# Opening of a two-block transformer kernel: the order of four modulation quarters and two projection pieces, one quarter summed by two engines, and one sum ahead of an eviction

## The reference, cut to what matters

```
cond_act = jax.nn.silu(c)
ada = (cond_act @ w_ada + b_ada)[:, None, :]
sh1, sc1, g1, sh2, sc2, g2 = jnp.split(ada, 6, axis=-1)
u = layer_norm(x) * (1 + sc1) + sh1
proj = u @ w_in + b_in
```

## Time and profile before

| what | value |
|---|---|
| median of 3 runs | 2474.4 us (2473.87 to 2475.06) |
| the profiled execution: time | 2474.91 us |
| its span, first to last instruction | 2472.9 us |
| mean granted TensorE clock | 0.986 |
| TensorE matmul busy | 2322.6 us (94%) |
| VectorE busy | 1017.7 us (41%) |
| ScalarE busy | 356.3 us (14%) |
| chain that ended last | TensorE 73%, DMA 20%, VectorE 3%, ScalarE 2% |

### The profile page before, as it was taken

The page is one execution under the profiler, slowest core; times in us unless marked ns, Lnnn a source line. Parts: engine busy times, 40 slices in busy tenths (PEclk is TensorE's granted clock), DMA queues, the critical chain, the costliest instruction groups (busy, mean ns, idle before and its releaser), DMA issues.

```text
span 2472.9 us, 26320 instructions
## 1 busy us (share of the span) xinstructions
PE 2322.6 (94%) x10448; PEld 1373.8 (56%) x10448; DVE 1017.7 (41%) x2212; ACT 356.3 (14%) x725; POOL 31.8 (1%) x54
## 2 busy tenths in 40 slices
PE   6999999999999999999998998988899989989997
PEld 5878688458878685467554333333397533333332
DVE  4254656767556567223743111111245521111112
ACT  1211111001211110101532111111100011111111
POOL 0100000002000000000000000000000000000000
PEclk9999999999999999999998999999999989999999
DMA  9644868856267688532045999999954369999996
GB/s 313 255 153 171 306 248 291 305 193 234 98 248 257 218 326 303 187 119 85 35 185 228 430 429 429 428 429 428 417 197 170 122 241 429 429 428 429 428 429 290
DMA packets 160900, 701.04 MB, mean 283 GB/s; under 512 B 6064, under 2 KB 15536, under 8 KB 135216
## 3 DMA queue, kind: packets, MB, share of 16 engines
q1 hardware_dynamic: 158512, 691.49, 70.9%
q0 software_dynamic: 2304, 8.39, 1.0%
HBM read 694.61 MB, written 5.24 MB: 283 GB/s over the span
## 4 chain that ended last, share of the span: by engine, by line
PE 73%; DMA 20%; DVE 3%; ACT 2%; issue 1%; SPq 1%; DVEq 0%; ACTq 0%
PE banks L615 72%; DMA ring<-in_exp_w_down_dram 19%; ACT UT L1406 1%; DMA ring<-in_w_ada_dram 1%; PE banks L680 0%; DVE acc L1790 0%; PE banks L748 0%; DVE acc L1763 0%; ACT arena L1613 0%; SPq L2587 0%; DVE arena L2220 0%; DVE arena L2213 0%; DVE X L1872 0%; PE banks L1153 0%; PE banks L995 0%
## 5 line engine op out<-in xcount | busy, mean ns | idle before, releaser
L615 PE MATMUL banks<-ring,arena 128*64 128x512 f32 (+2 forms) x3776 | 976.4, 593 | 80.0 <-DVE arena L2220 29.1
L615 PE MATMUL banks<-UT,ring 128*128 128x256 f32 (+1 forms) x3696 | 729.3, 356 | 7.0 <-ACT UT L1406 3.9
L615 PEld LDWEIGHTS banks<-ring,arena 128*64 128x64 f32 (+1 forms) x3776 | 360.5, 147 | 660.2 <-issue 619.5
L615 PEld LDWEIGHTS banks<-UT,ring 128*128 128x128 f32 x3696 | 623.7, 192 | 86.9 <-issue 15.9
L1790 DVE SCALAR_TENSOR_TENSOR acc<-ring,cact,acc 128x512 f32<-128x512 f32 x280 | 212.7, 760 | 9.9
L2212 DVE TENSOR_TENSOR arena<-arena,banks 128x512 f32<-128x512 f32 x32 | 33.9, 1061 | 442.0 <-PE banks L615 442.0
L1586 ACT ACTIVATE arena<-banks 128x512 f32<-128x512 f32 (+1 forms) x96 | 65.2, 679 | 799.0 <-PE banks L615 759.9
L615 PE MATMUL banks<-arena 64*128 64x512 f32 (+4 forms) x752 | 139.5, 433 | 4.6 <-ACT arena L1453 2.8
L615 PEld LDWEIGHTS banks<-arena 64*128 64x128 f32 (+2 forms) x752 | 69.1, 172 | 77.9 <-issue 62.1
L2220 DVE TENSOR_TENSOR arena<-banks,acc 128x512 f32<-128x512 f32 x32 | 22.2, 692 | 208.7 <-PE banks L615 208.7
L615 PE MATMUL banks<-ring,XN 128*128 128x512 f32 (+1 forms) x192 | 73.0, 540 | 0.0
(11 more groups left out here) (249 smaller groups left out, 1453.1 us busy)
## 6 DMA issues: line engine op xcount, KB each, us to landing
ring<-in_exp_w_gate_dram SPq DMA_DIRECT2D x64, 2048.0 KB, 22.1
ring<-in_exp_w_up_dram SPq DMA_DIRECT2D x64, 2048.0 KB, 25.2
ring<-in_exp_w_down_dram SPq DMA_DIRECT2D x64, 2048.0 KB, 17.1
ring<-in_w_in_dram SPq DMA_DIRECT2D x26, 2048.0 KB, 14.0
ring<-in_mod_w_dram SPq DMA_DIRECT2D x24, 2048.0 KB, 9.2
ring<-in_w_ada_dram SPq DMA_DIRECT2D x20, 2048.0 KB, 8.5
ring<-in_w_up_dram SPq DMA_DIRECT2D x16, 2048.0 KB, 9.4
ring<-in_w_down_dram SPq DMA_DIRECT2D x16, 2048.0 KB, 9.3
```

The source lines that it names most:

```text
L615: return nc.tensor.matmul(o, lhs, rhs, start=start, stop=stop)
```

## The change

Five edits, all in the opening:

1. `plan_pieces` orders the first six pieces ada 0, in 0, ada 1, ada 2, in 1, ada 3.
2. Quarter 1 is summed by two engines. VectorE takes blocks 0 to 3 (one TENSOR_SCALAR, three that accumulate, no share of ScalarE). TensorE takes blocks 4 to 7: after one product of four columns with zeros that opens the bank, 16 products with a 128 x 128 block of the weights as the stationary operand and a column of `cact` as the moving one. The four products with ones are added to the same bank.
3. VectorE sums quarters 2 and 3 one after the other, and only then evicts quarter 2 and quarter 3. ScalarE, too, computes shares 2 and 3 before its blocks of quarters 2 and 3.
4. The parts on TensorE come in another order between the four `first_modulation` calls.
5. A quarter's slot is released when its bank is full, not when the sum in `acc` is.

```diff
     for n in range(FIRST_STEPS):
         out.append(("ada", 0, n))
-        if n < 2:
-            out.append(("in", 0, n))
+        if n in (0, 2):
+            out.append(("in", 0, n // 2))
...
                 bank = take(pe, g, n % 2)
+                if n == 1:
+                    pe.wait_ge(cact_ready, 1)
+                    w = piece(pe, ("ada", 0, n)).rearrange("p (k q c) -> p k q c", q=4, c=P)
+                    mm(bank[:, 0:4], zero, C("ones", 0, 4), True, False)
+                    for k, q in itertools.product(range(KC // 2, KC), range(4)):
+                        mm(bank[:, q:q + 1], w[:, k, q, :], cact[:, k:k + 1], False, False)
                 pe.wait_ge(acc_ready, n + 1)
                 for q in range(4):
-                    x = mm(bank[:, q:q + 1], acc[:, n % 2, q * P:q * P + P], C("ones", 0, 1), True, True)
+                    x = mm(bank[:, q:q + 1], acc[:, n % 2, q * P:q * P + P], C("ones", 0, 1), n != 1, n != 1 or q == 3)
                 finish(x, g)
-                released[("ada", 0, n)] = (acc_ready, n + 1)
+                release(("ada", 0, n), g)
...
                     first_modulation(1)
-                    for n, i in ((1, 0), (1, 1), (0, 2), (0, 3), (1, 2), (1, 3)):
+                    for i in (0, 1):
+                        part(1, i)
+                    first_modulation(2)
+                    for n, i in ((0, 2), (0, 3), (2, 0), (2, 1), (1, 2), (1, 3), (2, 2)):
                         part(n, i)
-                    first_modulation(2)
-                    for i in range(3):
-                        part(2, i)
                     first_modulation(3)
                     part(2, 3)
                     for i in range(4):
...
-                    for n in range(FIRST_STEPS):
-                        if n:
-                            first_share(n)
+                    for n in (0, 1):
+                        first_quarter(n)
+                    for n in (2, 3):
+                        first_share(n)
+                    for n in (2, 3):
                         first_quarter(n)
...
-            def first_quarter(n):
+            def first_sum(n):
 
                 w = piece(dve, ("ada", 0, n)).rearrange("p (k n) -> p k n", n=512)
                 dst = acc[:, n % 2, :]
-                dve.wait_ge(share_ready, n + 1)
-                link(V.scalar_tensor_tensor(out=dst, in0=w[:, 0, :], scalar=cact[:, 0:1], in1=share[:, n % 2, :],
-                                            op0=ALU.mult, op1=ALU.add))
-                for k in range(1, KC - 1):
+                if n == 1:
+                    link(V.tensor_scalar(dst, w[:, 0, :], cact[:, 0:1], None, ALU.mult))
+                else:
+                    dve.wait_ge(share_ready, (1, 0, 2, 3)[n])
+                    link(V.scalar_tensor_tensor(out=dst, in0=w[:, 0, :], scalar=cact[:, 0:1], in1=share[:, n % 2, :],
+                                                op0=ALU.mult, op1=ALU.add))
+                own = KC // 2 if n == 1 else KC - 1
+                for k in range(1, own):
                     x = V.scalar_tensor_tensor(out=dst, in0=w[:, k, :], scalar=cact[:, k:k + 1], in1=dst,
                                                op0=ALU.mult, op1=ALU.add)
-                    if k < KC - 2:
+                    if k < own - 1:
                         link(x)
                 x.then_inc(acc_ready, 1)
+
+            def first_quarter(n):
+
                 g = ("ada", 0, n, "x")
...
-                    for n in range(FIRST_STEPS):
+                    for n in (0, 1):
+                        first_sum(n)
+                        first_quarter(n)
+                    for n in (2, 3):
+                        first_sum(n)
+                    for n in (2, 3):
                         first_quarter(n)
                     rotary_angles()
```

## The result

| | before | with the change |
|---|---|---|
| median | 2474.16 us (14 runs, 2471.84 to 2475.2) | 2480.96 us (14 runs, 2479.39 to 2481.77) |
| ratio | | 1.0027, 95% interval 1.002 to 1.0034 |
| profiled execution | 2474.91 us | 2480.07 us |
| its span | 2472.9 us | 2477.9 us |
| ScalarE goes on after the last part | 67.14 us | 72.04 us |

What follows compares the result with a forecast made beforehand. TensorE bounds the kernel, 73% of the chain, so the opening's delay reaches the end. Part (2,0) at 51.6 and the remaining parts give 70.5, plus 1.7 clock 72.2 against 67.1: +5.1 on 2474.4, 2479.5 us; range 2476.0 to 2482.5.

Steps and rivals of the forecast that it cites:

- The landings: Opening's transfers: third quarter lands near 32.2 us, piece in 1 near 38.2, the fourth quarter still last at 44.2.
- Second quarter: TensorE's narrow products: clock falls at 31.2 us, bank full at 36.6 instead of 35.0.
- Third quarter: VectorE's third sum runs 38.4 to 43.9 us; TensorE reaches part (2,0) between 48.8 and 52.7.
- 1 to 3: Sign of being right: TensorE waits 1 to 3 us for ScalarE's `UT` before part (2,0).
- The deciding step: Fourth sum ahead of third's eviction on VectorE: sum ends 50.6 us, part (2,0) starts 51.6, ten parts left.
- Clock at the gap: TensorE idle up to 2.8 us before part (2,0), then half clock: costs 1.7 us, bounds 0 and 3.6.
- rival 1: Clock holds over the gap before part (2,0): +3.4 us, 2477.8 us; chance 0.12.
- Rival 4: Opening loses 5 us but something later absorbs part; half of it, 2477 us; chance 0.08.
- Rival 3: Fourth quarter lands early, VectorE's sums run straight on: -0.6 us, 2473.8 us; chance 0.05.
- Rival 2: All 42 narrow products at half clock delay the third quarter: +6.7 to +8.5 us, say 2481.9 us; chance 0.13.
- The sum: Opening ends at 72.2 us against 67.1: +5.1 us, bounds +3.4 and +7.0; forecast 2479.5 us.

Runs made afterwards that it cites:

- e9: Against e5: first six pieces in the order of before (in 1 ahead of the third quarter); median 2478.5 us, ratio to before 1.0019.
- e5: Against e1: TensorE takes two of the second quarter's eight row blocks instead of four, VectorE six; median 2471.9 us, ratio to before 0.9993.
- e6: Against the changed kernel: eight products with zeros on TensorE between parts (0,3) and (2,0); median 2480.2 us, ratio to before 1.0027.
- e3: Against the changed kernel: piece in 1 queued behind the fourth quarter, which so lands earlier; median 2476.8 us, ratio to before 1.0006.
- e1: Against the changed kernel: third quarter evicted before the fourth is summed, ScalarE's blocks and shares likewise; median 2473.8 us, ratio to before 0.9995.
- e2: Against the changed kernel: parts (1,2) and (1,3) ahead of (2,0) on TensorE; median 2476.0 us, ratio to before 1.0007.
- e4: Against the changed kernel: first six pieces in the order of before, in 1 ahead of the third quarter; median 2479.2 us, ratio to before 1.0019.
- a0: The changed kernel measured again with no edit; median 2479.5 us, ratio to before 1.0015.
- e7: Against e1: second quarter summed whole by VectorE with ScalarE's share, without the 17 extra TensorE products; median 2473.0 us, ratio to before 0.9997.
- e8: Against e5: zeros that open two of the four banks moved behind the parts of quarter 0; median 2473.5 us, ratio to before 0.9999.
- e6b: Against the changed kernel: ten products with zeros on TensorE between parts (0,3) and (2,0); median 2479.3 us, ratio to before 1.0024.

## Why the prediction was right

*The landings.* Forecast 44.2 for the fourth quarter; ScalarE's wait for it ended at 44.76. The execution as a whole began 0.5 us later (first transposes at 14.73 against 14.22), and that 0.5 is in the 4.9. From there the landing came when it was forecast. e9 and e5 show the third quarter's: 38.75 in the old order, and in the new one before ScalarE asks for it at 33.6.

*Second quarter.* Forecast a full bank at 36.6, with the clock falling in the narrow products; measured 34.29 + 1.84 = 36.13, and a fall near 32.2 with TensorE busy throughout. The 32 new records took 3.71 us at full clock (e6) and 4.72 in the change. That narrow products are dearer at half clock, is borne out: 8 records take 1.03 us in e6 and 1.84 in the change. That they make the clock fall is not a rule: in e6 and e3 all 42 ran at full clock, and the clock fell only in the wait of 0.95 us behind them. The Trainium skill (TensorE: Matmul & The Clock Gate, LDWEIGHTS (loading the stationary operand)) gives one figure for a load, its columns over 1.2, and names no level of the clock. Read as the prediction read it, as the same at either level, it does not hold here: the rows of the same eight weight loads are 0.97 us in e6 and 1.83 in the change.

*Third quarter.* Forecast 38.4 to 43.9 for the sum; measured 37.76 to 43.24. Arrival at part (2,0): forecast 48.8 to 52.7, measured 47.97, earlier than either bound. So the gap is 3.92 us, where the prediction had at most 2.8 and "1 to 3" among its signs.

*The deciding step.* Forecast a fourth sum from 45.0 to 50.6 and part (2,0) at 51.6; measured 45.59 to 51.0 and 51.89. That the order on VectorE and the two parts behind the wait are the loss, and not the narrow products, e1 and e2 show by undoing one of them each, e1 in the medians too.

*Clock at the gap.* The term was 1.7 us with bounds 0 and 3.6. Measured against the 8.8 us without a gap: 1.8 and 2.7 in two executions of the change (gaps of 3.92 and 3.84), 3.0 in e6 (3.11), 0 in e4 (1.55, with the fall just ahead of the gap instead). This is the term that was sized low, at the short end of what happens, and it was read from shorter gaps than the one that came; rival 1 (it holds) happened only where the gap was shorter than forecast.

*Behind the opening.* Nothing was absorbed: the rest was 2405.8 and 2405.9, and the medians are not closer together than the openings. That the two agree to 0.1 us is luck, since the rest of other profiles differs by up to 5.8 us. Rival 4 falls. Rival 3 needs a landing at 39 to 41, and only an edit (e3) brought it there, to 38.47. Rival 2 fell in both profiles of the change, since the bank was full before 37.9.

*The sum.* +5.1 forecast, +4.9 in the opening and +5.0 in the span; +6.8 in the medians of 14 runs and +5.2 in those of a0 (2479.5 against 2474.3). The mechanism is the forecast one, but so close a number is in part luck: counted from the first transposes, the opening of that profile is 4.4 us longer. Up to about 1 us of what the first medians have above the forecast can be the clock at the gap; the rest stays open.

## What to carry to other kernels

Before an engine with a fixed list is given a step earlier, ask what that step waits for, and who waits for what is now behind it: here a sum that waits for the last transfer was put ahead of an eviction of 0.2 us, behind which ten of 16 parts stood. Ahead of a wait, put all work that doesn't need it, whatever order the numbers of the parts suggest. And measure an edit in the schedule in which it is to work: the new order of pieces was worth nothing beside the late eviction (e4) and 7 us without it (e9).

## What was not expected of the hardware

The time behind the opening is the same code in all these kernels, and yet the rest lies between 2402.1 and 2407.9 us. The granted clock tells part of it. The first line is that of 16 wide records right behind a group of narrow ones near 115 us; the others are stretches (from:to, us, busy, clock, DMA share, GB/s). In e1:

```profile
116.52 5.41 PE L615 MATMUL banks<-UT,ring 128*128 128x256 f32 x16
110.00:125.00 15.00, 15.00 (x66) 0.89 0.41 141
1225.00:1250.00 25.00, 24.26 (x138) 0.86 0.20 85
```

and in e9:

```profile
121.49 3.72 PE L615 MATMUL banks<-UT,ring 128*128 128x256 f32 x16
110.00:125.00 15.00, 15.00 (x75) 1.00 0.40 138
1225.00:1250.00 25.00, 23.90 (x156) 1.00 0.20 85
```

At both places TensorE is busy without a gap of note and works narrow or small products (at 113 us on 64 and 4 partitions, at 1234 us with one column), and whether the clock falls there differs between executions. Six profiles have no fall near 115 us (before, the change, a0, e4, e6, e9); the eight others have one, and it costs them 1.3 to 1.7 us. Those eight are all the runs of edited kernels in which the last part came before 70 us, so part of what an edit gains in the opening is lost again there; why the clock falls in these and not in before (67.14), no run shows. The first run of e5, e7, e8 and e9 have no fall at 1235 us, the others have one. e5's two profiles show what it does to a single time: 0.7 us apart at the last part, 4.6 us apart in the span. So a gain of 2 or 3 us is read from the place of the edit in the trace and from medians of many runs, not from one execution's total; and as e6b shows, the place of the edit alone is not enough either.
